# A DeltaNet scan over chunks of 128 tokens, restated in 64-token sub-chunks with two heads stacked on the partitions

## The chip, the cores and the metric

The kernel runs on one core of one Trainium2 chip. The metric is the device time of one launch in microseconds: the median of three runs before the change is 1980.43 us (1977.72 to 1982.88).

## The reference, cut to what matters

One layer of a hybrid trunk over a prompt of 1024 tokens and a sample of 32 tokens (width 1024): a joint input projection, eight gated DeltaNet heads of 64 with a causal convolution, eight stick-breaking attention heads, an output projection, an MLP of 4096 and a gated embedding. The change touches the DeltaNet rule alone:

```python
gcum = jnp.cumsum(gc, axis=-1)
decay = jnp.exp(jnp.where(causal, gcum[..., :, None] - gcum[..., None, :], -jnp.inf))
a_mat = jnp.where(strict, jnp.einsum('nbhid,nbhjd->nbhij', kb, kc) * decay, 0.0)
sol = lax.linalg.triangular_solve(a_mat + jnp.eye(l), rhs, left_side=True, lower=True, unit_diagonal=True)
qk = jnp.where(causal, jnp.einsum('nbhid,nbhjd->nbhij', qc, kc) * decay, 0.0)
def step(s, xs):
    v_new = u_i - jnp.einsum('bhld,bhde->bhle', w_i, s)
    o = (jnp.einsum('bhld,bhde->bhle', q_i * jnp.exp(g_i)[..., None], s)
         + jnp.einsum('bhij,bhje->bhie', qk_i, v_new))
    s = (s * jnp.exp(g_last)[..., None, None]
         + jnp.einsum('bhld,bhle->bhde', k_i * jnp.exp(g_last[..., None] - g_i)[..., None], v_new))
    return s, o
```

Each head carries a 64x64 state from chunk to chunk. Within a chunk the keys form a lower triangular matrix that must be inverted. The chunk length is free: any length gives the same result. All of it is float32.

## The kernel before, in words

The program runs in stages, one after another on all engines: input projection and convolution, stick-breaking attention (prompt, then sample), the DeltaNet scan, then output projection, MLP, embedding. The weight products take their operands as pairs of rounded halves, three PE passes each (tile_product); they are the part after the scan.

The scan works on CHUNKS = 9 chunks: chunk 0 is the sample (32 tokens), 1 to 8 are the prompt in pieces of 128 tokens. Tokens stand on partitions in the matrices of a chunk (128x128 for each of eight heads), channels in the transposed keys and queries (head pairs, 64 rows each). The order is written out by hand for each engine in a loop over i from -3, in which stages of several chunks are interleaved:

- chunk i+3: squares, square sums (square_sums, PE L2106), logs and norms on ACT, unit_norms (DVE L1581), decay_differences (DVE L1570, one operation per head);
- chunk i+2: products of keys (key_products, PE L2112), key_matrix on DVE (L1599), decayed keys and queries (L1589, L1590 on DVE, L933, L934 on POOL), turns of keys and values (L2135, L2137), products of queries (L2112 again). SP writes the key matrix to DRAM (blocks_out, L733) and reads back its 16x16 diagonal blocks as 64 lanes (L737). DVE inverts these on lanes (lanes_begin, lanes_middle, lanes_end, L1630 to L1666). SP scatters the inverses and their transposes into scratch of zeros (L742, L743) and reads whole matrices d_t and d_x back (L747, L750);
- chunk i+1: three levels double the inverted blocks from 16 to 128. A level is a product of the key matrix with d_t (L2207, last one L2256), a mask on ACT (L1244, L1258, L1273), a product that completes d_t (L2213) and one that completes d_x (L2220, last one L2264);
- chunk i: products_of_state (L2152, L2154), rest_of_values (DVE L1680), solved_values (PE L2171), new_values (DVE L1686), state_change (PE L2181), new_state (DVE L1691), outputs (PE L2190), norm of outputs, turn_outputs (PE L2200), rounding into act_hi and act_lo.

Iterations -3 to -1 are the prologue. In the last one the first tile of the output projection is interleaved. On PE every product of a head is one matmul with float32 operands; the profile shows two records for each, and one for a transpose. SP handles all loads of the scan in program order in one queue: blocks_out(i+2), sums_in(i+3), blocks_in(i+2), z_in, conv_v_in, conv_qk_in. A wait at one of them holds all behind it.

PSUM banks: key and query products put even heads into one bank and odd heads into the next (group, value and output use h % 2).

## Time and profile before

| | |
|---|---|
| median of 3 runs | 1980.43 us (1977.72 to 1982.88) |
| the profiled execution, its span | 1980.4 us |
| PE busy | 1826.4 us (92%) |
| DVE busy | 806.4 us (41%) |
| ACT busy | 522.2 us (26%) |
| POOL busy | 620.3 us (31%) |
| scan | about 648 to 992.7 us |

Busy time counts an engine's instructions from start to end; a busy PE is not a PE at its peak. In a timeline each row is a group of like instructions: start, length, engine, line, operation, outputs and inputs, shapes, and in brackets the idle time before it and what ended it. The clock column is the granted TensorE clock as a share of 2.4 GHz; it has two levels, 0.50 (1.2 GHz) and 1.00. Most of the profiled time lies after the scan, where PE streams weight products.

### The profile page before, as it was taken

The page shows a single profiled execution, that of the slowest core. Times are in us where ns is not written, and L with a number is a line of the kernel's source. Part 1 is how long each engine was busy: PE and PEld are TensorE (multiplying, and loading weights), DVE is VectorE, ACT ScalarE, POOL GpSimd, SP SyncE. Part 2 cuts the span into 40 slices and gives each one's busy share as a digit, 9 for nine tenths or more (in the row PEclk, how much of TensorE's full clock was granted, in tenths as well). Part 3 has the DMA queues.
Part 4 walks back from the last instruction along what each step waited for, and adds up shares of the span by engine and source line. Part 5 has one row for each costly group of instructions (what it writes and reads, how often), then busy time and mean ns, then how long its engine had stood idle before and what let it go on. Part 6 is the DMA issues. An engine that isn't in the chain of part 4 may idle for free.

```text
span 1980.4 us, 29352 instructions
## 1 busy us (share of the span) xinstructions
PE 1826.4 (92%) x12590; PEld 1728.3 (87%) x12590; DVE 806.4 (41%) x1031; ACT 522.2 (26%) x987; POOL 620.3 (31%) x337
## 2 busy tenths in 40 slices
PE   4999999989998468887999999999999999999998
PEld 4989989977776258777899999999999999999898
DVE  5552125558996455656213322212222222225432
ACT  4222122337776233443213201010101010103211
POOL 4132223312340112123053434443444344332430
PEclk9999999999999578888799999999999999999999
DMA  5121322132003443342232111111111111111121
GB/s 166 44 71 39 108 66 76 55 118 67 1 1 107 105 102 94 89 107 53 52 93 75 43 53 44 43 43 54 43 43 43 54 43 43 43 53 61 51 61 46
DMA packets 197663, 126.50 MB, mean 64 GB/s; under 512 B 39024, under 2 KB 190980, under 8 KB 197540
## 3 DMA queue, kind: packets, MB, share of 16 engines
q1 hardware_dynamic: 188112, 111.69, 19.5%
q10 hardware_dynamic: 9428, 13.02, 1.8%
q8 instruction: 96, 1.57, 0.3%
q14 instruction: 27, 0.22, 0.0%
HBM read 100.07 MB, written 24.62 MB: 63 GB/s over the span
## 4 chain that ended last, share of the span: by engine, by line
PE 75%; DVE 14%; issue 4%; ACT 4%; DMA 2%; POOL 1%; SPq 0%; ACTq 0%; DVEq 0%; POOLq 0%
PE psum L2074 41%; PE psum L1892 8%; PE psum L2388 5%; PE psum L1861 3%; PE psum L1862 3%; PE psum L1863 3%; DVE act_lo_plain L1527 3%; PE psum L2207 2%; DVE act_hi_plain L1528 2%; DVE area L1630 1%; PE psum L2106 1%; PE psum L1944 1%; PE psum L2407 1%; DVE area L1467 1%; DVE act_lo L1764 1%
## 5 line engine op out<-in xcount | busy, mean ns | idle before, releaser
L2074 PE MATMUL psum<-act_hi,w_round 128*128 128x352 f32 x1920 | 369.8, 326 | 0.5 <-DVE act_lo L1764 0.5
L911 POOL TENSOR_TENSOR w_round<-w_plain,ones 128x1024 fp32r<-128x1024 f32 x80 | 173.8, 2173 | 533.1 <-DMA w_plain<-in_w_up_dram 231.2
L2074 PEld LDWEIGHTS psum<-act_hi,w_round 128*128 128x128 f32 x1920 | 321.8, 190 | 1.4 <-DVE act_lo L1764 0.8
L2074 PE MATMUL psum<-hid_hi,w_round 128*128 128x352 f32 x1344 | 260.0, 324 | 0.4 <-DVE hid_lo L1794 0.4
L2074 PEld LDWEIGHTS psum<-hid_hi,w_round 128*128 128x128 f32 x1344 | 224.9, 188 | 0.7 <-DVE hid_lo L1794 0.7
L1771 DVE TENSOR_TENSOR area<-psum,area 128x1056 f32<-128x1056 f32 x72 | 90.5, 1257 | 311.3 <-PE psum L2074 311.3
L2074 PE MATMUL psum<-act_lo,w_round 128*128 128x352 f32 x960 | 208.0, 325 | 0.0
L912 POOL TENSOR_TENSOR w_round<-w_plain,w_round 128x1024 fp32r<-128x1024 f32 x80 | 198.5, 2481 | 6.3
L1386 ACT ACTIVATE hid_hi<-area 128x1056 fp32r<-128x1056 f32 x28 | 30.4, 1088 | 592.5 <-DVE area L1787 592.5
L1861 PE MATMUL psum<-w_round,act_hi 128*128 128x256 f32 (+1 forms) x576 | 166.3, 289 | 6.6 <-POOLq L863 3.6
L2074 PEld LDWEIGHTS psum<-act_lo,w_round 128*128 128x128 f32 x960 | 164.4, 189 | 0.0
L1862 PE MATMUL psum<-w_round,act_hi 128*128 128x256 f32 (+1 forms) x576 | 163.6, 284 | 0.0
L1863 PE MATMUL psum<-w_round,act_lo 128*128 128x256 f32 (+1 forms) x576 | 162.6, 282 | 0.0
L2074 PE MATMUL psum<-hid_lo,w_round 128*128 128x352 f32 x672 | 144.8, 324 | 0.0
L1787 DVE SCALAR_TENSOR_TENSOR area<-psum,area 128x1056 f32<-128x1056 f32 x32 | 40.2, 1257 | 240.1 <-PE psum L2074 235.1
L860 POOL TENSOR_TENSOR w_round<-w_plain,ones 128x2048 fp32r<-128x2048 f32 x14 | 50.5, 3609 | 254.2 <-PE psum L1863 163.2
L2074 PEld LDWEIGHTS psum<-hid_lo,w_round 128*128 128x128 f32 x672 | 114.0, 188 | 0.0
L1861 PEld LDWEIGHTS psum<-w_round,act_hi 128*128 128x128 f32 (+1 forms) x576 | 104.6, 182 | 7.9 <-issue 3.7
L1892 PE MATMUL psum<-act_hi,w_round 128*128 128x352 f32 x576 | 109.1, 324 | 0.0
L1863 PEld LDWEIGHTS psum<-w_round,act_lo 128*128 128x128 f32 (+1 forms) x576 | 105.0, 182 | 0.4
L1862 PEld LDWEIGHTS psum<-w_round,act_hi 128*128 128x128 f32 (+1 forms) x576 | 104.5, 181 | 0.4
L1527 DVE TENSOR_TENSOR_SCAN act_lo_plain<-act_lo_plain,w_plain 128x128 f32<-128x128 f32 (+7 forms) x64 | 88.3, 1380 | 23.5 <-ACT act_hi_plain L1096 22.7
(294 smaller groups left out, 2911.0 us busy)
## 6 DMA issues: line engine op xcount, KB each, us to landing
w_plain<-in_w_up_dram SPq DMA_DIRECT2D x32, 512.0 KB, 4.1
w_plain<-in_w_down_dram SPq DMA_DIRECT2D x32, 512.0 KB, 3.4
w_plain<-in_w_in_dram SPq DMA_DIRECT2D x14, 1024.0 KB, 5.6
conv_scratch<-area ACTq DMA_DIRECT2D x12, 512.0 KB, 2.7
w_plain<-decay_scratch SPq DMA_DIRECT2D x9, 512.0 KB, 3.5
area<-t_scratch SPq DMA_DIRECT2D x9, 512.0 KB, 4.2
area<-x_scratch SPq DMA_DIRECT2D x9, 512.0 KB, 5.5
area<-in_x_prompt_dram SPq DMA_DIRECT2D x8, 512.0 KB, 3.2
```

The lines of the kernel that those rows point to most:

```text
L860: own.link(pool.tensor_tensor(hi, w_raw[:, slot, :], ones[:, 0:1].to_broadcast([P, BLK]), ALU.mult))
L911: own.link(pool.tensor_tensor(hi, ring_raw(n), ones[:, 0:1].to_broadcast([P, RB]), ALU.mult))
L912: pool.tensor_tensor(lo, ring_raw(n), hi.bitcast(F32), ALU.subtract).then_inc(ring_split, 1)
L1527: own.link(dve.tensor_tensor_scan(back, back, starts, 0.0, ALU.mult, ALU.max))
L1771: dve.tensor_tensor(h3, chunks_of(bank_set(tile)), h3, ALU.add).then_inc(drained, 1)
L1787: dve.scalar_tensor_tensor(out=by_chunk(wide[:, n % 2, :]), in0=chunks_of(bank_set(tile)), scalar=0.0, in1=by_chunk(wide[:, 2, :]), op0=AL ...
L1861: pe.matmul(out, hi[:, k, cols], w_h(k), start=(k == 0), stop=False)
L1862: pe.matmul(out, hi[:, k, cols], w_l(k), start=False, stop=False)
L1863: last = pe.matmul(out, lo[:, k, cols], w_h(k), start=False, stop=(k == K - 1))
L1892: last = pe.matmul(bank(base + c)[0:rows, 0:CH], w(k), a[:, k, CH * c:CH * (c + 1)], start=(k == 0 and w is lhs_hi and a is hi), stop=(k = ...
L2074: last = pe.matmul(bank(bank_set(tile) + c)[:, 0:CH], w(k), a(k)[:, CH * c:CH * (c + 1)], start=(begins and k == ks[0] and w is w_h and a ...
L2388: last = pe.matmul(bank(c)[:, 0:CH], w(k), a[:, k, CH * c:CH * (c + 1)], start=(k == 0 and w is w_h and a is act_hi), stop=(k == KT - 1 an ...
```

## The change

A chunk of 128 tokens (or of 32, padded to 64) is split into sub-chunks of HD = 64 tokens, g = 0 and 1. Two heads are stacked on the partitions (index u), so that a matrix tile is [128, m, 64] with m = 4g + k: half u of the partitions holds head 2k + u. Every product of a head takes rows of half u and writes rows of half u of one bank (place). Elementwise operations on matrices of 128x1024 become 128x512. The inverse has two levels (16 to 32 on 64x64 products, 32 to 64 on 32x32 products); the third is gone. The state advances once per sub-chunk, step(q, g), twice per iteration, and alternates between two buffers. Turns become products with the identity, two per 128x128 piece and half. decay_differences is split: the subtraction runs on POOL (raw_differences), DVE takes the minimum with a mask. Several tiles have three buffers in place of two, d_gb and d_cn two in place of one. key_matrix is made one iteration earlier (chunk i+3), output norms one later (chunk i-1). d_t and d_x come back in four transfers (two halves each) under one semaphore, blocks_back, for which first_matrices waits. z comes in four transfers. SP's order changes: sums first, blocks_out last; the ring of weight blocks 2 to 4 is loaded in iteration 6 in place of after the scan, and POOL splits three of its blocks in the last iterations in place of two. For the sample, token sums and betas are laid out for the halves by small products before the scan.

```diff
-        d_dt = carve(area, 0, 2, H, P)
+        d_dt = carve(area, 0, 2, M2, HD)
...
+        def step(q, g):
+            return 2 * q - 1 + g if q else 0
+        def steps_to(q):
+            return 2 * q + 1
+        STATES = steps_to(CHUNKS - 1)
+        def state(n):
+            return d_s[:, (n - 1) % 2] if n else d_sin[:, 0]
+        def next_state_of(n):
+            return d_s[:, n % 2] if n else d_sin[:, 1]
...
+                sp.dma_start(scratch, zeros).then_inc(scratch_cleared, 16)
             sp.wait_ge(g_stored, 16)
             sums_in(0)
             sp.wait_ge(kc_turned, 2)
@@ -725,13 +749,15 @@
             sp.wait_ge(so_split, 2)
             for u in range(2):
                 sp.wait_ge(z_stored[u], 16 * NTT)
+            sp.dma_start(d_sin[:, 0], state_of["in"]).then_inc(s_loaded, 16)
 
             def blocks_out(q):
 
-                n = size(q)
                 sp.wait_ge(at_made, q + 1)
-                sp.dma_start(at_scratch[0:n, :, 0:n], d_at[0:n, q % 2, :, 0:n]).then_inc(at_dumped, 16)
-                sp.wait_ge(at_dumped, 16 * (q + 1))
+                for u in range(2):
+                    sp.dma_start(at_scratch[u, 0:HD, 0:mats(q)], d_at[HD * u:HD * (u + 1), q % 3, 0:mats(q)])\
+                      .then_inc(at_dumped, 16)
+                sp.wait_ge(at_dumped, 32 * (q + 1))
                 if q:
                     sp.wait_ge(scattered, 32 * q)
                 sp.dma_start(d_lane[:, 0:LB * LB].rearrange("l (r c) -> l r c", c=LB), at_lanes).then_inc(gathered, 16)
@@ -742,46 +768,45 @@
                 sp.dma_start(t_lanes, d_lane_t.rearrange("l (r c) -> l r c", c=LB)).then_inc(scattered, 16)
                 sp.dma_start(x_lanes, d_lane[:, 0:LB * LB].rearrange("l (r c) -> l r c", c=LB)).then_inc(scattered, 16)
...
-                if 0 <= i + 2 < CHUNKS:
-                    blocks_out(i + 2)
-                if 1 <= i + 3 < CHUNKS:
-                    sums_in(i + 3)
-                if i < 0:
-                    if i + 4 >= 2:
-                        conv_v_in(i + 4)
-                    conv_qk_in(i + 4)
-                    if i == -1:
-                        z_in(0)
+                if i + 4 < CHUNKS:
+                    sums_in(i + 4)
+                if i >= 0:
+                    if i == 0:
+                        sp.wait_ge(consts_made, 6)
+                    z_in(i)
                 if 0 <= i + 2 < CHUNKS:
                     blocks_in(i + 2)
-                if i >= 0:
-                    if i + 1 < CHUNKS:
-                        z_in(i + 1)
-                    if i + 4 < CHUNKS:
-                        conv_v_in(i + 4)
-                        conv_qk_in(i + 4)
+                if 2 <= i + 4 < CHUNKS:
+                    conv_v_in(i + 4)
+                if i + 4 < CHUNKS:
+                    conv_qk_in(i + 4)
+                if i + 3 < CHUNKS:
+                    blocks_out(i + 3)
                 if i == 1:
                     sp.wait_ge(s_new, 2)
-                    sp.dma_start(state_of["sample"], d_sin).then_inc(s_stored, 16)
-            sp.wait_ge(s_new, 1 + CHUNKS)
...
+            def raw_differences(q):
+                m = mats(q)
+                pool.wait_ge(gb_loaded, 32 * (q + 1))
+                pool.wait_ge(at_made, q)
+                gc = gc_all[:, chunk(q), 0:m].unsqueeze(2).to_broadcast([P, m, HD])
+                tt(d_db[:, 0:m], d_gb[:, q % 2, 0:m], gc, ALU.subtract).then_inc(dtb_made, 1)
...
-                for h in range(H):
-                    last = dve.scalar_tensor_tensor(out=d_db[0:n, h, 0:n], in0=d_gb[0:n, h, 0:n],
-                                                    scalar=gc_all[0:n, chunk(q), h:h + 1], in1=causal[0:n, 0:n],
-                                                    op0=ALU.subtract, op1=ALU.min)
-                last.then_inc(diff_made, 1)
+                m = mats(q)
+                dve.wait_ge(dtb_made, 2 * q + 1)
+                bound = causal[:].unsqueeze(1).to_broadcast([P, m, HD])
+                tt(d_db[:, 0:m], d_db[:, 0:m], bound, ALU.min).then_inc(diff_made, 1)
...
+            def place(b, u, m):
+                return bank(b)[half(u), HD * m:HD * (m + 1)]
...
+            def keys_on_state(q, g):
+                n = step(q, g)
+                pe.wait_ge(kg_made, q + 1)
+                pe.wait_ge(s_new, n + 1)
+                if n == 0:
+                    pe.wait_ge(s_loaded, 16)
+                for k in range(WT):
+                    for u in range(2):
+                        last = pe.matmul(place(5, u, k), d_kg[half(u), q % 3, WT * g + k], state(n)[half(u), k],
+                                         start=True, stop=True)
+                last.then_inc(ks_ready, 1)
...
+            def second_matrices(q):
+                pe.wait_ge(t16_made, q + 1)
+                for m in range(mats(q)):
+                    for u in range(2):
+                        top, rest = slice(HD * u, HD * u + 32), slice(HD * u + 32, HD * (u + 1))
+                        last = pe.matmul(bank(0)[rest, HD * m:HD * m + 32], d_at[top, q % 3, m, 32:HD],
+                                         d_t[top, q % 2, m, 0:32], start=True, stop=True)
+                last.then_inc(m_ready, 1)
```

PE's loop after the change (code of the new kernel):

```python
            for i in range(-3, CHUNKS + 1):
                now, two, final = 0 <= i < CHUNKS, 0 < i < CHUNKS, i == CHUNKS - 1
                if now:
                    keys_on_state(i, 0)
                if final:
                    pe.wait_ge(m_made, level(i, 1))
                    pe.wait_ge(qt_made, CHUNKS)
                    pe.wait_ge(x_made, level(i, 1))
                    heads_part([WT], True)
                if 0 <= i + 1 < CHUNKS:
                    first_matrices(i + 1)
                if now:
                    solved_values(i, 0)
                if 0 <= i + 1 < CHUNKS:
                    first_inverse(i + 1)
                if now:
                    state_change(i, 0)
                    outputs(i, 0)
                if i + 3 < CHUNKS:
                    square_sums(i + 3)
                if two:
                    keys_on_state(i, 1)
                if final:
                    heads_part([WT + 1], False)
                if i >= 1:
                    turn_outputs(i - 1)
                if 0 <= i + 1 < CHUNKS:
                    second_matrices(i + 1)
                if two:
                    solved_values(i, 1)
                if 0 <= i + 2 < CHUNKS:
                    turn_keys(i + 2)
                    query_products(i + 2)
                if 0 <= i + 1 < CHUNKS:
                    second_inverse(i + 1)
                if two:
                    state_change(i, 1)
                    outputs(i, 1)
                if final:
                    heads_part([WT + 2, WT + 3], False)
                if i + 3 < CHUNKS:
                    key_products(i + 3)
```

How the rows of an iteration move. PE, a steady iteration before, from the products of the state (L2152) on; names: 2207 level products, 2213 d_t, 2220 d_x, 2171 solved values, 2181 state change, 2190 outputs, 2106 square sums.

```order
L2152 MATMUL psum<-area 128x64 x8
L2154 MATMUL psum<-area 128x64 x8
L2112 MATMUL psum<-w_plain 128x128 x8
L2207 MATMUL psum<-area 128x128 x8
L2171 MATMUL psum<-area 128x64 x8
L2213 MATMUL psum<-area 128x128 x8
L2220 MATMUL psum<-area 128x128 x8
L2181 MATMUL psum<-area 64x64 x8
L2207 MATMUL psum<-area 128x128 x8
L2190 MATMUL psum<-area 128x64 x8
```

The same place now: state product (L2163), first matrices (L2219), solved values (L2172), d_t and d_x of the first level (L2227, L2233), state change (L2181), outputs (L2193, L2197), square sums (L2116), and the state product of the second sub-chunk.

```order
L2163 MATMUL psum<-area 64x64 x8
L2219 MATMUL psum<-area 64x64 x16
L2172 MATMUL psum<-area 64x64 x8
L2227 MATMUL psum<-area 64x64 x16
L2233 MATMUL psum<-area 64x64 x16
L2181 MATMUL psum<-area 64x64 x8
L2193 MATMUL psum<-area 64x64 x8
L2197 MATMUL psum<-area 64x64 x8
L2116 MATMUL psum<-w_plain,halves 128x512 x2
L2163 MATMUL psum<-area 64x64 x8
```

Products of 128 columns are gone but for the square sums, which moved between the two state steps, ahead of the second state product; the key products moved from here to the iteration's end.

SP's queue, a steady iteration before (L733 dump, L737 gather, L742 and L743 scatter, L747 and L750 returns):

```order
L733 DMA at_scratch<-area 128x8x128
L737 DMA area<-at_scratch 64x16x16
L651 DMA w_plain<-decay_scratch 128x1024
L742 DMA t_scratch<-w_plain 64x16x16
L743 DMA x_scratch<-area 64x16x16
L747 DMA area<-t_scratch 128x8x128
L750 DMA area<-x_scratch 128x8x128
L657 DMA area<-z_scratch 128x512
L644 DMA w_plain<-conv_scratch 128x4x128
L637 DMA w_plain<-conv_scratch 128x8x128
```

And now (L768, L769 scatter; L774, L779 returns; L758 dump; L763 gather):

```order
L671 DMA w_plain<-decay_scratch 64x512 x2
L682 DMA area<-z_scratch 64x4x64 x4
L768 DMA t_scratch<-w_plain 64x16x16
L769 DMA x_scratch<-area 64x16x16
L774 DMA area<-t_scratch 64x8x64 x2
L779 DMA area<-x_scratch 64x8x64 x2
L660 DMA w_plain<-conv_scratch 128x4x128
L653 DMA w_plain<-conv_scratch 128x8x128
L758 DMA at_scratch<-area 64x8x64 x2
L763 DMA area<-at_scratch 64x16x16
```

Dump and gather moved behind the scatter and returns of the chunk before. Ten transfers became seventeen, and those that carry the matrices of heads or z move rows of 64 elements.

## Rows read from the trace of the kernel before

**Rows 1.** The profile's page, header and granted clock of PE in 40 slices
```profile
span 1980.4 us, 29352 instructions
...
PEclk9999999999999578888799999999999999999999
```

**Rows 2.** Busy time by stretch: PE, PEld, DVE, ACT, POOL, then clock, DMA share, GB/s
```profile
680.00:720.00 40.00, 18.29 (x154) 14.51 (x152) 17.28 (x31) 7.45 (x14) 5.88 (x5) 0.61 0.46 119
...
789.37:823.92 34.55, 29.39 (x257) 25.70 (x257) 20.04 (x42) 13.62 (x29) 6.46 (x6) 0.85 0.37 98
...
992.70:1040.00 47.30, 47.29 (x301) 47.16 (x302) 5.61 (x5) 7.41 (x8) 23.70 (x11) 0.96 0.29 81
```

**Rows 3.** Timeline of PE: start us, us, engine, line, operation, records, idle before
```profile
740.55 1.11 PE L2152 MATMUL psum<-area 64*128 64x64 f32 x16
...
808.68 1.14 PE L2264 MATMUL psum<-area 64*64 64x64 f32 x16
...
882.61 2.05 PE L2207 MATMUL psum<-area 128*128 128x128 f32 x16
...
890.43 0.69 PE L2181 MATMUL psum<-area 128*64 128x64 f32 x16 [0.36 <-DVE area L1686]
...
947.46 1.97 PE L2152 MATMUL psum<-area 64*128 64x64 f32 x16
```

**Rows 4.** Timeline of PE, groups at the low clock
```profile
801.01 3.75 PE L2106 MATMUL psum<-w_plain,halves 128*128 128x512 f32 x4 [3.13 <-DVE area L1704]
...
943.71 1.96 PE L2264 MATMUL psum<-area 64*64 64x64 f32 x16
```

**Rows 5.** Busy time of single microseconds around the pause, columns as rows 2
```profile
800.00:801.00 1.00, 0.00 (x0) 0.02 (x1) 0.96 (x3) 0.00 (x0) 0.00 (x0) 0.50 0.14 17
...
807.00:808.00 1.00, 1.00 (x18) 0.93 (x17) 0.20 (x1) 0.41 (x2) 0.00 (x0) 1.00 1.20 296
```

**Rows 6.** Timeline of PE, sample attention and its last turn
```profile
640.92 0.65 PE L2023 MATMUL psum<-w_plain,act_hi_plain 128*32 128x64 f32 x32
...
645.56 0.65 PE L2052 MATMUL psum<-ident,act_hi_plain 32*64 32x32 f32 x16 [0.34 <-ACT act_hi_plain L1167]
```

**Rows 7.** Timeline of DVE, parts of the iterations at 789 and 824
```profile
795.59 1.01 DVE L1630 TENSOR_TENSOR area<-area 64x512 f32<-64x512 f32 x1
...
800.78 2.18 DVE L1570 SCALAR_TENSOR_TENSOR area<-w_plain,gc_all,causal 128x128 f32<-128x128 f32 x8
...
820.77 0.68 DVE L1589 TENSOR_TENSOR area<-w_plain 64x512 f32<-64x512 f32 x1 [4.07 <-ACT w_plain L1224]
821.47 1.67 DVE L1590 TENSOR_TENSOR area<-w_plain 64x512 f32<-64x512 f32 x1
...
825.03 0.07 DVE L1658 MEMSET area<- 64x16 f32 x1
...
825.91 0.42 DVE L1691 TENSOR_TENSOR area<-psum,w_plain 128x256 f32<-128x256 f32 x1
...
827.50 0.28 DVE L1634 TENSOR_REDUCE area<-area 64x32 f32<-64x128 f32 x1
```

**Rows 8.** Timeline of ACT, the four first masks
```profile
818.19 1.48 ACT L1244 ACTIVATE area<-psum,odd 32x128 f32<-32x128 f32 x4 [5.75 <-PE psum L2207]
```

**Rows 9.** Timeline of SP's DMA issues: scatter and first return
```profile
799.57 0.59 SPq L742 DMA_DIRECT2D t_scratch<-w_plain  x1
...
802.82 0.36 SPq L747 DMA_DIRECT2D area<-t_scratch  x1
```

**Rows 10.** DMA issues of the scan, median us from issue to landing
```profile
area<-t_scratch SPq DMA_DIRECT2D x9, 512.0 KB, 4.2
area<-x_scratch SPq DMA_DIRECT2D x9, 512.0 KB, 5.5
...
at_scratch<-area SPq DMA_DIRECT2D x8, 512.0 KB, 3.2
...
area<-at_scratch SPq DMA_DIRECT2D x9, 64.0 KB, 2.7
```

More of the change, by code:

```diff
@@ L2260, in last_inverse @@
[L2260 to L2286 removed]
+                pe.wait_ge(at_made, q + 1)
@@ new lines, in outputs @@
+            def outputs(q, g):
+                n = step(q, g)
+                pe.wait_ge(qg_made, q + 1)
+                pe.wait_ge(qt_made, q + 1)
+                if q:
+                    pe.wait_ge(on_read, q)
+                for k in range(WT):
+                    for u in range(2):
+                        pe.matmul(place(6, u, WT * g + k), d_qg[half(u), q % 3, WT * g + k], state(n)[half(u), k],
+                                  start=(g == 0 and k == 0), stop=False, skip_group_check=True)
+                for k in range(WT):
+                    for u in range(2):
+                        last = pe.matmul(place(6, u, WT * g + k), d_qt[half(u), q % 3, WT * g + k], d_vn[half(u), k],
+                                         start=False, stop=True, skip_group_check=True)
+                if g == subs(q) - 1:
+                    last.then_inc(o_made, 1)
@@ new lines, in first_inverse @@
+            def first_inverse(q):
+                pe.wait_ge(m_made, level(q, 0))
+                for m in range(mats(q)):
+                    for u in range(2):
+                        last = pe.matmul(place(0, u, m), d_x[half(u), q % 3, m], d_m[half(u), m], start=True, stop=True)
+                last.then_inc(t_ready, 1)
+                if q:
+                    pe.wait_ge(x_made, level(q - 1, 1))
+                for m in range(mats(q)):
+                    for u in range(2):
+                        last = pe.matmul(place(1, u, m), d_m[half(u), m], d_x[half(u), q % 3, m], start=True, stop=True)
+                last.then_inc(x_ready, 1)
```

851 lines of the change are left out of this document (377 added, 474 removed).

## The prediction

> **What bounds the kernel now.** Read first the page's header and clock line [rows 1], then the busy time in stretches [rows 2]. PE is busy in nearly all of 992.7 to 1040 us and stays so until the end; the change does not touch that part, it only starts earlier or later. The DeltaNet scan fills 648 to 992.7 us. Its steady part repeats: PE is busy 29.4 of 34.6 us of one iteration (85%), DVE 20.0, ACT 13.6, POOL 6.5 [rows 2]. The prologue is another matter: between 680 and 720 us PE is busy 18.3 of 40 us, since there each step waits for the one before. So two numbers matter: the length of an iteration, which PE's own work sets now, and the latency of the chain through the blocks' inverses, which sets the prologue. Iteration 1 starts at 740.55 us and iteration 7 at 947.46 (both are the first products with the state) [rows 3], which is 34.5 us per iteration.
>
> The PE timeline [rows 3] gives prices. A float32 product is two records. At the full clock a group of 16 records takes 2.05 us where both operands are 128 wide (128 ns a record), 1.14 us for 64x64 products on one tile (71 ns), and 0.69 us for 64-column products whose column halves alternate (43 ns). Two halves that alternate thus run beside each other. At half clock (0.50, which is 1.2 GHz) the 64x64 group takes 1.96 us, 122 ns a record [rows 4].
>
> The clock: PE is idle for 3.13 us before the square sums at 801.01 (after DVE L1704); the granted clock is 0.50 at 800 and 1.00 from 807 on, with PE busy since 801.01 [rows 4, 5]. It loses this in each iteration.
>
> **The change, part by part.**
>
> *Price of a product.* All products of a head become 64x64 on diagonal tiles, rows half u onto columns half u, u alternating. That form isn't in the scan before. Bounds: 71 ns if the tiles run one after another, 35 ns if they run in pairs (half of 71, and near the 43 of the alternating column halves). I take 36 at full clock and 61 at half (half of 122). The nearest row is the small turn at 645.56: four row groups alternating with two column halves, 16 records in 0.65 us at a clock of 0.50, so 40 ns [rows 6]; the attention's 32-column tiles take 20 ns [rows 6]. Both speak for pairs, and the first also writes one bank from two row groups.
>
> *Products per iteration.* Before, 252 records, most with 128-wide operands, and 4 for the square sums. Now: keys, queries, first matrices, both first inverses and turned outputs 32 each, turned keys and values 64, state products, solved values and state change 16 each for two sub-chunks, outputs 64; together 416 records of 64x64, and 64 of 32x32 for the second level (a third level is gone). PE: 416 x 0.036 + 64 x 0.030 + 1.9 (half of 3.75) = 18.8 us at full clock, 416 x 0.061 + 64 x 0.040 + 3.75 = 31.7 at half [rows 4]. The transposes cost more (two records per 64x64 piece instead of one per 128x128), all else less.
>
> A rule speaks against so many small products. The Trainium skill (TensorE: Matmul & The Clock Gate, What happens when you issue a matmul) says that with hardware decoding off the sequencer spends about 62 ns on each MATMUL. By it 484 records would take 30.0 us an iteration as an estimate; the sum goes by the rows instead. The trace disagrees: 20 ns a record at 640.92 [rows 6].
>
> *DVE.* decay_differences falls from 2.18 to 0.7 us (one operation of 512 elements, as 0.68 for the one at 820.77), the decayed queries from 0.68 + 1.67 to 0.7, the key and query matrices to half their size and time; three value and state steps run twice at 0.42 [rows 7]. The inverse of the 16-blocks on lanes is untouched. DVE goes from 20.0 to about 18, POOL from 6.5 to about 4.5, ACT stays under 13. None of them fills an iteration.
>
> *What is late next.* PE no longer bounds; a loop does. first_matrices(i+1) now waits for all four returning transfers of d_t and d_x. From that moment, F, in PE's and DVE's order: first matrices 32 x 0.061 = 1.95 (half clock, as PE has just waited); masks on ACT 1.48 [rows 8]; both first inverses 3.90; state change 16 x 0.061 = 0.98; the clock is back, outputs 1.15; square sums 1.9; second state product 0.6; rest_of_values on DVE 0.42; decay_differences 0.70; the lanes' first half 2.4 (825.03 to 827.78, less the 0.42 of the state step in it); new_values 0.42; the lanes' last half 3.95, from 795.59 to the scatter issued at 799.57 [rows 7, 9]; then SP: returns issued 802.82, so 3.25 [rows 9]; returns 4.5 (landing was 4.2 and 5.5 for 512 KB each [rows 10]; now four transfers of 128 KB, of as many pieces, each issued some 0.4 after the other: between 3.3 and 5.9). Together 27.6. To this, 0.7 for a dozen hand-overs (0.02 to 0.1 each in the timelines), and 1.0 because POOL's product falls into the lanes: of two DVE products of one size, 0.68 and 1.67, the second runs beside POOL [rows 7]. **29.3 us** per iteration instead of 34.5. The other loop, at_made through dump and gather (3.2 and 2.7 to land [rows 10], some 6.5 with the issues) to the lanes, has 10 us of slack, as the lanes begin 14 us after F. The recurrence itself is two rounds of 3 x 0.6 on PE and 3 x 0.42 on DVE, some 8 us; it doesn't decide.
>
> *Steady part.* Six intervals from F(2) to F(8); the last has no square sums and no differences: 5 x 29.3 + 26.6 = 173 instead of 207: 34 us saved.
>
> *Prologue.* SP's order now puts the next loads ahead of the waits for blocks. Key matrix 0 is made at about 654; dump and gather 6.5, lanes 7.5, scatter and returns 7.8 give F(0) = 676; matrices, masks, transposed product, first_transposed and differences 5.4, lanes 7.5, returns 7.8 give F(1) = 697; the same with state step and contention gives F(2) = 724 instead of 740.55: 16.5 us saved.
>
> *End.* Iteration 7 has no lanes: 16.5 us from F(8). Iteration 8 has two state steps but the same 12 products of the output tile between them, and the turning of outputs at the end: 20.5. From F(8) to the full stream of PE 37 us, against 45.2 before (947.46 [rows 3] to 992.7 [rows 2]): 8 to 8.5 saved. The weight blocks 2 to 4 are now loaded in iteration 6; PE didn't wait for them before, so nothing comes of it, nor from POOL splitting one block more.
>
> **Sum**: 34 (steady) + 16.5 (prologue) + 8.5 (end) = 59. The profiled execution has a span of 1980.4 us, the same as the median of the runs (1980.43), so the forecast is 1980.4 - 59 = **1921 us**.
>
> **Rivals.**
> 1. *Shorter loop*: the clock stays full and the returns take 3.3 us. F to F: 24.5 to 25 us, end near 1890. Against it: PE idles two or three times in each iteration (before F, at the masks, before the key products), some 7 of 29 us, and a 3 us pause cost the clock before.
> 2. *Half clock all through the iteration*: the loop takes 33 (outputs, square sums, state product and the hand-overs double), end near 1948. For it: the prologue, busy 46%, has a clock of 0.61 [rows 2]. Against it: at half clock PE would have 31.7 us of work in 33, and so dense a PE is granted the full clock.
> 3. *Diagonal tiles run one after another*, the rival on the other side. Two row groups write the same bank in every product of the new code (place() has no bank by half, before group() and value() had h % 2). At 71 ns PE has 416 x 0.071 + 64 x 0.043 + 1.9 = 34.2 us at full clock, and the loop through F, the masks and the key products leaves it idle for 4 to 5 more: 38 to 40 an iteration. Then 5 x 39 + 36 = 231, F(2) at 728, and an end of 43 us: 1002 instead of 992.7, so 1990. It decides from about 69 ns a record on, where the iteration reaches 38 us. The Trainium skill (TensorEngine Tiling (Array Packing), Restrictions and Gotchas) states that different row tiles cannot access the same PSUM bank simultaneously. By that rule the pairs would be impossible here and the time that of this rival; the turn at 645.56 speaks against it.
> 4. *Another wait takes PE's place at the same length*: the returns take 11 us instead of 4.5, being small pieces that queue with the loads of z and convolution. The loop is then 35.8 and F(2) comes at 743.5, so PE's full stream starts at 743.5 + 5 x 35.8 + 33 + 37 = 992.5. That is no change: within 0.3%, which is about what a measurement of this kernel can tell from none. Against it: 512 KB came back in 4.2 to 5.5 [rows 10].
>
> **How the numbers follow.** Forecast's case (loop of 27 to 31.5) 0.58, at 1905 to 1935. Rival 1 0.13, rival 2 0.16, rival 3 0.08, rival 4 0.05. Faster: 0.58 + 0.13 + 0.16 = 0.87; same 0.05; slower 0.08. The range goes from rival 1's time to a little beyond rival 2's, 1890 to 1950, and leaves out rivals 3 and 4 and the far end of rival 1.
>
> **What would show it.** The 64x64 groups of 16 records at 0.58 us or less at full clock (over 0.9 would be rival 3); PE busy for 60 to 75% of an iteration with a clock between 0.6 and 0.85; before first_matrices a PE wait of 1 to 3 us, released by the transfer of x_scratch; iterations of 27 to 31.5 us; iteration 1 near 724; the stages after the scan as long as before. The prediction is wrong if DVE fills the iteration, if first_matrices doesn't wait for DMA, or if the later stages change.

## The result, and the profile after

The changed kernel takes **1904.86 us** (median of 4 runs, 1901.27 to 1906.32), the kernel before 1979.88 beside it (4 runs, 1977.72 to 1982.88). The ratio is 0.9622, with a 95% interval of 0.9609 to 0.9636: 75 us, or 3.8%, faster. The forecast was 1921 in a range of 1890 to 1950, so the sign and the range hold, and the gain is 16 us larger than the sum said. The profiled execution took 1903.72 us. These are the header of its page and the granted clock of PE, to be read against [rows 1]:

```profile
span 1902.0 us, 33199 instructions
...
PEclk9999999998999878787999999999999999999999
```

The clock line dips to 7 in the scan and no longer to 5. Busy time by stretch (columns as in rows 2) shows how the balance moved:

```profile
680.00:720.00 40.00, 26.25 (x556) 21.78 (x555) 23.41 (x54) 16.08 (x37) 8.01 (x7) 0.80 0.32 66
...
778.43:806.02 27.59, 20.96 (x485) 18.79 (x485) 16.28 (x36) 10.72 (x24) 5.63 (x5) 0.75 0.38 85
806.02:834.49 28.47, 20.49 (x485) 18.46 (x485) 16.28 (x36) 10.71 (x24) 5.62 (x5) 0.74 0.38 86
834.49:860.71 26.22, 18.79 (x485) 16.76 (x485) 16.19 (x36) 10.71 (x24) 4.58 (x4) 0.83 0.36 75
```

The last three are whole iterations, from one first_matrices to the next. Against the 34.55 us of [rows 2], PE is busy 19 to 21 us in place of 29.4, that is 72 to 76% of the iteration, DVE 16.3 in place of 20.0. No engine fills an iteration: PE is waiting for something, and its timeline names it. Columns: start us, us, engine, line, operation, records, idle before and its releaser.

```profile
724.70 1.98 PE L2219 MATMUL psum<-area 64*64 64x64 f32 x32 [3.79 <-DMA area<-x_scratch]
...
806.02 1.97 PE L2219 MATMUL psum<-area 64*64 64x64 f32 x32 [2.24 <-DMA area<-x_scratch]
...
809.56 1.97 PE L2227 MATMUL psum<-area 64*64 64x64 f32 x32 [0.72 <-ACT area L1286]
811.33 1.92 PE L2233 MATMUL psum<-area 64*64 64x64 f32 x32
813.03 0.77 PE L2181 MATMUL psum<-area 64*64 64x64 f32 x16
...
814.67 1.98 PE L2116 MATMUL psum<-w_plain,halves 128*128 128x512 f32 x4
816.58 0.68 PE L2163 MATMUL psum<-area 64*64 64x64 f32 x16
817.10 1.10 PE L2208 MATMUL psum<-ident,area 64*64 64x64 f32 x32
818.13 0.69 PE L2241 MATMUL psum<-area 32*32 32x32 f32 x32
...
828.41 1.97 PE L2125 MATMUL psum<-area 64*64 64x64 f32 x32 [4.01 <-DVE area L1593]
...
860.71 1.98 PE L2219 MATMUL psum<-area 64*64 64x64 f32 x32 [2.70 <-DMA area<-x_scratch]
...
888.55 1.97 PE L2219 MATMUL psum<-area 64*64 64x64 f32 x32 [7.38 <-DMA area<-x_scratch]
...
893.08 1.10 PE L2233 MATMUL psum<-area 64*64 64x64 f32 x32
894.02 0.63 PE L2181 MATMUL psum<-area 64*64 64x64 f32 x16
```

L2219 is first_matrices; F(q) is the moment at which it starts for chunk q. F(2) is at 724.70 and F(8) at 888.55: six intervals of 27.3 us on average, each entered after a wait of PE for the transfer of x_scratch. Prices stand here too. Thirty-two records on the diagonal tiles take 0.94 us from one group's start to the next at full clock (L2233 starts at 893.08, L2181 at 894.02), which is 29 ns a record; at half clock 1.77 us (809.56 to the start of L2233 at 811.33), 55 ns. The 32x32 products take 0.62 us for 32 records (from L2241's start to that of the next group at 818.75), 20 ns.

DVE and SP, the rest of the same loop (columns as above):

```profile
817.31 0.42 DVE L1692 TENSOR_TENSOR area<-area,psum 128x256 f32<-128x256 f32 x1 [1.94 <-PE psum L2163]
817.65 0.68 DVE L1585 TENSOR_TENSOR area<-area,causal 128x512 f32<-128x512 f32 x1
818.29 0.07 DVE L1670 MEMSET area<- 64x16 f32 x1
...
824.73 0.37 DVE L1678 COPY w_plain<-area 64x256 f32<-64x256 f32 x1
```
```profile
825.12 0.60 SPq L768 DMA_DIRECT2D t_scratch<-w_plain  x1
825.76 0.67 SPq L769 DMA_DIRECT2D x_scratch<-area  x1
828.39 1.27 SPq L774 DMA_DIRECT2D area<-t_scratch  x2
829.71 2.08 SPq L779 DMA_DIRECT2D area<-x_scratch  x2
```

DVE waits for the second state product, does the value step, the minimum of the differences and the lanes without a pause, SP scatters at 825.12 and issues the returns at 828.39, and PE goes on at 834.49. The returns take 6.1 us from first issue to F, and the four issues alone 3.4. This is the longest of the six intervals: in the others the returns take 5.0 to 5.5 us and, but for one, the issues 2.6.

**Where the 75 us are.** Marks are F(2), F(8) and the first turn of the last outputs (L2327 at 918.89 now, L2339 at 992.71 before, the start that [rows 2] has for PE's full stream); the kernel before is read at its first products with the state, 740.55 and 947.46. The steady six intervals take 163.9 us in place of 206.9 [rows 3]: 43.0. F(2) stands at 724.70 in place of 740.55: 15.9. From F(8) to the mark it is 30.3 us in place of 45.3: 14.9. Together 73.8. What is left of the 78.4 us between the two spans, 4.6, lies behind the mark, where PE has the same products in both kernels: 987.7 us before, 983.1 now. Part of the 78.4 is a difference between executions, since the medians differ by 75.0 only. A time is 1.7 to 1.8 us longer than its span in every run, so the traced execution of the kernel before took about 1982.1, 2.2 over its median. But the traces of all thirteen kernels with the change, those of the experiments below included, have 980.6 to 983.6 us behind the mark. There is one trace of the kernel before, so whether the change has a share in the 4.6 is open.

### The profile page after: what moved, and what is told of

It is laid out like the page before. It is cut to its first block, busy times and chain, and to the rows that moved or that the text cites. A ratio compares the mean times of both kernels' runs of the same rounds, so it can differ in the third digit from the quotient of the medians.

```text
span 1902.0 us, 33199 instructions
## 1 busy us (share of the span) xinstructions
PE 1738.7 (91%) x14512; PEld 1648.3 (87%) x14512; DVE 767.2 (40%) x988; ACT 502.4 (26%) x970; POOL 615.0 (32%) x340
## 4 chain that ended last, share of the span: by engine, by line
PE 73%; DVE 13%; DMA 4%; issue 4%; ACT 2%; SPq 2%; POOL 1%; ACTq 0%; DVEq 0%; POOLq 0%
PE psum L2090 42%; PE psum L1902 8%; PE psum L2376 5%; DVE act_lo_plain L1544 3%; PE psum L1871 3%; PE psum L1872 3%; PE psum L1873 3%; DVE act_hi_plain L1545 2%; DVE area L1642 1%; DMA area<-x_scratch 1%; DMA x_scratch<-area 1%; PE psum L1954 1%; PE psum L2395 1%; DVE area L1482 1%; DVE area L1646 1%
```

## Experiments

Each kernel ran in 4 executions beside the kernel before. Ratios are to that kernel, with their 95% intervals.

### The same tile in a row

The theory was that pairing of diagonal tiles carries the gain, the rival that smaller matrices do. The edit reorders the products inside each group and nothing else (one loop of several that are changed alike):

```diff
-                for k in range(WT):
-                    for u in range(2):
+                for u in range(2):
+                    for k in range(WT):
```

> The changed kernel with its products in another order: in each group all eight (or four) products of half u = 0, then those of u = 1, in place of alternating. Same products, same waits. Theory (the two diagonal tiles run beside each other, and that is what made PE cheap): 16 records of 64x64 take 1.14 us at full clock instead of 0.47, PE has about 34 us of work per iteration and sets its length again, 37 to 40 us; total 1970 to 1995 us, the whole gain gone. Rival (small products are cheap in any order, and the gain is from the shorter waits and SP's new order): 16 records stay under 0.6 us, total within 10 us of 1905.

Measured: 1957.36 us (1954.79 to 1959.0), 0.9884 [0.9867, 0.9900], 52.5 us slower than the change. PE timeline of this kernel:

```profile
802.06 2.98 PE L2227 MATMUL psum<-area 64*64 64x64 f32 x29 [0.59 <-ACT area L1286]
...
813.50 1.67 PE L2208 MATMUL psum<-ident,area 64*64 64x64 f32 x29
815.10 1.09 PE L2241 MATMUL psum<-area 32*32 32x32 f32 x32
```

and its busy time over one iteration (columns as in rows 2):

```profile
797.19:831.57 34.38, 30.62 (x484) 28.58 (x484) 16.62 (x37) 10.71 (x24) 4.98 (x5) 0.75 0.30 68
```

With the same 484 records PE is busy 30.6 of 34.4 us. A record costs 55 ns at full clock (29 of them from 813.50 to 815.10) and 96 at half (29 from 802.06 to 804.84, where the next one starts), in place of 29 and 55. So diagonal tiles that alternate run at the pace of pairs, though both write the same bank. PE still waits for x_scratch, 0.4 to 2.2 us before F(3) to F(7), so the loop is the same one with longer groups in it: from F to the state change it takes 10.2 us, in place of 5.5 to 7.0. The time lies between the two expectations; theory had priced a record at 71 ns. So 52.5 of the 75 us are the pairing, by its order alone, and about 22 come with products on one tile too: this kernel is 1.2% faster than the one before. How these 22 divide between smaller matrices and the new order in SP's queue wasn't taken apart. The rival on the other side would have needed 69 ns a record; unpaired the tiles take 55 at full clock.

### Two waits of the loop, apart and together

In the loop read above, first_matrices needs only d_t, and the square sums stand ahead of the second state product for which DVE waits. The first edit gives the returns of d_x a semaphore of their own, for which first_inverse waits:

```diff
-                      .then_inc(blocks_back[q % 2], 16)
+                      .then_inc(x_back[q % 2], 16)
...
-                pe.wait_ge(blocks_back[q % 2], 64 * (q // 2 + 1))
+                pe.wait_ge(blocks_back[q % 2], 32 * (q // 2 + 1))
...
                 pe.wait_ge(m_made, level(q, 0))
+                pe.wait_ge(x_back[q % 2], 32 * (q // 2 + 1))
```

> The changed kernel with the returns of d_x under a semaphore of their own, waited for by first_inverse; first_matrices waits for d_t alone. Theory (the loop from the returned blocks through first_matrices, square sums, lanes, scatter and returns sets the iteration): first matrices start about 1.3 to 2.5 us earlier in each iteration, and 8 iterations give 10 to 18 us: 1887 to 1895. Rival (DVE's own work and its waits for PE set the iteration, and the wait for d_x only takes up slack): under 3 us.

The second puts square_sums(i + 3) behind solved_values(i, 1) in PE's order:

```diff
-                if i + 3 < CHUNKS:
-                    square_sums(i + 3)
                 if two:
                     keys_on_state(i, 1)
...
                     solved_values(i, 1)
+                if i + 3 < CHUNKS:
+                    square_sums(i + 3)
```

> The changed kernel with square_sums(i+3) on PE moved from ahead of the second state product to behind the second solved values. Theory (loop through the lanes): the second state product, and with it rest_of_values and the lanes, comes 1.9 us sooner; 5 steady iterations and the prologue's give 8 to 14 us: 1891 to 1897. Rival (the loop through norms, key matrix, dump and gather is as long): the later norms hold unit_norms, nothing is gained or up to 8 us lost.

> Both edits together: d_x waited for apart, square sums behind the second solved values. Alone they brought 10.5 and 9.4 us. Theory (both shorten one loop, at two places of it): they add, 1883 to 1888. Rival (they free the same slack, and another wait stops the second): 1891 to 1895.

Measured: d_x apart 1894.38 (1892.13 to 1901.09), 0.9580 [0.9558, 0.9602], 10.5 us under the change. Squares late 1895.42 (1894.99 to 1900.27), 0.9583 [0.9567, 0.9599], 9.4 under. Both 1886.64 (1885.48 to 1889.39), 0.9537 [0.9521, 0.9553], 18.2 under, so the two nearly add. All three lie in the range of their theory. PE timeline of the kernel with both (L2182 is the state change):

```profile
771.78 1.10 PE L2220 MATMUL psum<-area 64*64 64x64 f32 x32
...
796.65 1.15 PE L2220 MATMUL psum<-area 64*64 64x64 f32 x32 [0.65 <-DMA area<-t_scratch]
...
801.29 0.63 PE L2182 MATMUL psum<-area 64*64 64x64 f32 x16
...
820.77 1.15 PE L2220 MATMUL psum<-area 64*64 64x64 f32 x32 [0.43 <-DMA area<-t_scratch]
```

The intervals from F(2) to F(8) are 24.1 to 25.3 us, and before F(4) to F(7) the wait for the transfers is 0.65 us and less (1.9 before F(3), 5.9 before F(8)). Two edits that touch only the chain returns, first matrices, lanes made the run shorter, so that chain was the bound of the changed kernel.

The clock has a share in this. From F to the state change the chain runs on PE: 7.0 us at half clock (806.02 to 813.03), 4.6 at full clock (796.65 to 801.29). With both edits it takes 4.6 in four of the six intervals, in place of 5.5 to 7.0. That is 7.5 of the 15.1 us by which F(2) to F(8) is shorter, and with the squares alone it is 5.8 of 11.1. With d_x apart alone it is 0.2 of 5.8; there the returns take 3.7 to 4.2 us from first issue to F, and 7 us more are gained before F(2). So shorter pauses of PE seem to have given twice, by their own length and by the clock behind them; with one trace of each kernel the two can't be told fully apart.

### Keeping the clock up

The granted clock is 0.75 in an iteration of the change, and PE waits twice (4.0 us before the key products, 2.2 before the first matrices). The edit fills these places with products of ones into the free bank:

```diff
+            def fill(n):
+                for _ in range(n):
+                    pe.matmul(bank(0)[:, 0:P], halves[:], ones[:], start=True, stop=True)
...
+                if 2 <= i + 1 < CHUNKS:
+                    fill(8)
...
+                    if i > 0:
+                        fill(14)
```

> The changed kernel with extra products that nothing reads (ones by halves, 128x128, into bank 0) in PE's two pauses of each iteration: 14 before key_products, 8 before first_matrices. Theory (the pauses cost the clock, and first matrices, both first inverses and state change at 0.50 lie on the loop): granted clock over 0.95 in the scan, the loop shorter by 2.5 to 3.5 us an iteration, total 1885 to 1893. Rival (the clock falls anyway, or the fillers push what stands behind them by as much as they give): 1900 to 1915.

Measured: 1899.98 (1898.09 to 1901.48), 0.9598 [0.9582, 0.9614], 4.9 us under the change, and far less than expected. Busy time by stretch:

```profile
724.00:750.00 26.00, 21.72 (x517) 19.36 (x515) 15.98 (x36) 10.39 (x24) 5.00 (x5) 1.00 0.39 85
...
802.00:828.00 26.00, 21.60 (x528) 19.32 (x527) 15.81 (x36) 10.72 (x24) 5.29 (x5) 1.00 0.40 90
```

The clock is 1.00 in two of four such stretches, yet the six intervals from F(2) to F(8) take 158.1 us in place of 163.9. Of the loop's 27 us five to six are the returns, three the scatter and eight DVE, and their times didn't change with the clock. What did is the stretch from F to the state change, 7.8 us less over the six intervals, and 5.8 of it reached the steady part. The expectation had 2.5 to 3.5 us an iteration, as if this stretch ran at half clock throughout; in the changed kernel it did so in three of six. PE still waits 1.6 to 2.9 us for the transfer before F(3) to F(7), so the eight fillers ahead of the first matrices delay nothing.

### What comes next in the loop

Three further orders were tried on the kernel with both waits mended. First, output norms ahead of the first masks on ACT, and the normed output ahead of the first new values on DVE:

```diff
+                if i >= 1:
+                    output_norms(i - 1)
                 if 0 <= i + 1 < CHUNKS:
                     first_masks(i + 1)
```

> As the run before, and ACT's output_norms ahead of first_masks and squares, DVE's normed_output ahead of the first new_values, where DVE waits for PE. Theory (outputs wait for on_read, which stands behind squares and masks, and 1.4 us of DVE in the loop go into DVE's pause): 3 to 8 us below the run before. Rival (PE's outputs had no wait there, the loop does not pass through it): within 1 us of it.

Measured: 1883.28 (1879.87 to 1886.19), 0.9513 [0.9494, 0.9532], 4.9% under the kernel before and 21.6 us under the change: the fastest kernel of the study. Against the kernel it starts from it is 3.4 us, with intervals that overlap, so this last step isn't shown. The one trace of each doesn't bear out its mechanism either: F(2) to F(8) takes 149.8 us here and 148.7 there. One of its iterations by busy time (columns as in rows 2), and a wait in its DVE timeline, before the lanes, that the kernel it starts from didn't have in the steady part:

```profile
771.68:796.15 24.47, 16.44 (x484) 14.44 (x484) 17.32 (x38) 10.84 (x24) 5.71 (x5) 1.00 0.43 95
```

```profile
781.49 0.07 DVE L1671 MEMSET area<- 64x16 f32 x1 [1.92 <-DMA area<-at_scratch]
```

Then the lanes ahead of the second value step, on top of that:

> As the run before, and on DVE the lanes' first half ahead of the second rest_of_values, and decay_differences behind the lanes. Theory (the lanes are on the loop and wait only for program order, since the gathered blocks land about 6 us after first matrices start): lanes_made comes 2 to 4 us sooner per iteration, 8 to 16 us below the run before. Rival (the gather lands too late, or the second state step becomes the bound): 0 to 3 us, or slower.

Measured: 1889.39 (1888.42 to 1891.87), 0.9547 [0.9531, 0.9563], 6 us slower than without it. The PE and DVE timelines show why:

```profile
783.36 0.68 PE L2173 MATMUL psum<-area 64*64 64x64 f32 x16 [1.80 <-DVE area L1693]
...
788.32 1.97 PE L2151 MATMUL psum<-ident,area 64*64 64x64 f32 x32 [1.35 <-ACT w_plain L1253]
```
```profile
794.10 0.42 DVE L1704 TENSOR_TENSOR area<-psum,area 128x256 f32<-128x256 f32 x1 [6.00 <-PE psum L2182]
```

PE now waits for the value step that the lanes hold up, the square sums and turned keys behind it start later, and DVE stands 6.0 us for the state change. The lanes do end sooner: the scatter is issued 14.4 to 16.0 us after F, in place of 15.5 to 18.4. But F then comes 5.2 to 8.9 us after the first return is issued, with no wait for the transfer in these five of the six iterations, so PE's order bounds the loop there and no longer the returns. Fillers on top of it (ten and six) didn't help:

> As the run before, with unread products in PE's pauses (10 before key_products, 6 before first_matrices). Theory (the first fillers gained 5 and not 16 us because outputs then waited for normed_output, which is gone): now 6 to 14 us below the run before. Rival (the fillers stand in the way, as the pauses are shorter now): 0 to 5 us above it.

Measured: 1890.84 (1888.85 to 1894.08), 0.9561 [0.9545, 0.9577], 1.5 us above the kernel without them.

The wait for the gather was then attacked in SP's queue, on the fastest kernel:

```diff
-                if 2 <= i + 4 < CHUNKS:
-                    conv_v_in(i + 4)
-                if i + 4 < CHUNKS:
-                    conv_qk_in(i + 4)
                 if i + 3 < CHUNKS:
                     blocks_out(i + 3)
+                if 2 <= i + 4 < CHUNKS:
+                    conv_v_in(i + 4)
+                if i + 4 < CHUNKS:
+                    conv_qk_in(i + 4)
```

> g2_norms_early and, in addition, SyncE sends the dump of the key matrix and issues the gather ahead of the two convolution loads of the next chunk. In g2_norms_early the dump was issued at 771.75 us behind the two loads (0.62 and 0.51 us of issue) and the gather only at 777.82, 4.8 us behind the end of the dump's issue; VectorE then waited 1.92 us for the gather before the lane inverse. Theory (the gather is on the loop): the gather is issued 1.5 to 3 us earlier, VectorE's wait before the lane inverse goes, the loop shrinks from about 24.8 us by 0.5 to 1.5 us in each of some seven iterations, and the run takes 1873 to 1880 us. Rival (the convolution loads come late instead, since they now stand behind the wait for the dump; or the solved values' chain on TensorE is the bound): within 2 us of 1883.

Measured: 1900.11 (1898.19 to 1901.63), 0.9606 [0.9590, 0.9622]: 16.8 us slower, and outside both expectations. The SP timeline, then ACT and PE of the same kernel:

```profile
772.97 1.31 SPq L780 DMA_DIRECT2D area<-x_scratch  x2
781.15 1.27 SPq L759 DMA_DIRECT2D at_scratch<-area  x2
785.70 0.59 SPq L764 DMA_DIRECT2D area<-at_scratch  x1
786.34 0.66 SPq L661 DMA_DIRECT2D w_plain<-conv_scratch  x1
787.04 0.51 SPq L654 DMA_DIRECT2D w_plain<-conv_scratch  x1
```
```profile
793.46 1.06 ACT L1245 ACTIVATE w_plain<-w_plain 128x1024 f32<-128x1024 f32 x1 [9.24 <-DMA w_plain<-conv_scratch]
```
```profile
794.57 3.48 PE L2117 MATMUL psum<-w_plain,halves 128*128 128x512 f32 x4 [4.18 <-ACT w_plain L1245]
```

The dump waits for the key matrix until 781.15, and the loads now stand behind it in the one queue, though their data was written before the scan. The squares of the next chunk wait 9.24 us for them, the key matrix comes from those squares, and the next dump waits for the key matrix: by the order of the code this is a new loop through the queue, and these waits fit it. This was the named rival, but its price had been put at nothing.

### POOL beside the lanes

In the last interval of the change, F(7) to F(8), two tiny operations of the lanes take 0.95 and 2.20 us in place of 0.16. Each ends with the operation that POOL has beside it, at 871.49 and 873.93 where POOL's end at 871.47 and 873.90. DVE timeline of the change, and POOL's beside it:

```profile
870.54 0.95 DVE L1662 TENSOR_TENSOR area<-area 64x8 f32<-64x8 f32 x1
871.53 0.17 DVE L1663 TENSOR_TENSOR area<-area 64x8 f32<-64x8 f32 x1
871.73 2.20 DVE L1664 TENSOR_TENSOR area<-area 64x8 f32<-64x8 f32 x1
```
```profile
869.58 1.89 POOL L940 TENSOR_TENSOR w_round<-w_plain,ones 128x1024 fp32r<-128x1024 f32 x1
871.55 2.35 POOL L941 TENSOR_TENSOR w_round<-w_plain,w_round 128x1024 fp32r<-128x1024 f32 x1
```

The edit moves POOL's splits of weights one iteration later, on the changed kernel and on the one with the gather early:

```diff
-                if i >= CHUNKS - 3:
-                    split_ring(i - (CHUNKS - 3))
+                if i >= CHUNKS - 2:
+                    split_ring(i - (CHUNKS - 2))
...
-            for n in range(3, BLOCKS):
+            for n in range(2, BLOCKS):
```

> The changed kernel with the first pair of GpSimd splits of weights for the stage behind the scan moved from iteration 6 to iteration 7 (and the second from 7 to 8). In the changed kernel these two operations (1.89 and 2.35 us from 869.58) stand beside the lane inverse of chunk 8, in which one VectorE operation took 2.20 us instead of 0.16, and the first matrices of chunk 8 waited 7.38 us instead of 2.3 to 3.3. Theory (the two engines hold each other up there, and the lateness reaches TensorE's wait): the operation takes 0.16 to 0.3 us, the wait before the first matrices of chunk 8 is 3.5 to 5 us, and the run is 2 to 4 us shorter than the changed kernel, 1900 to 1903. Rival (the wait before chunk 8 is long because chunk 8's iteration has less work on TensorE, and the moved splits delay the stage behind the scan by as much): the operation is short, the run within 1 us of 1904.9.

> g5_gather_early with the first GpSimd split moved one iteration later as in x2_split_later. If both theories hold, their gains add: 1870 to 1877. If the splits' delay costs behind the scan what it saves in it, the same as g5_gather_early within 1.5 us.

Measured, on the change: 1902.46 (1900.33 to 1907.48), 0.9622 [0.9601, 0.9643]; on the other: 1899.87 (1897.71 to 1907.49), 0.9601 [0.9585, 0.9617]. DVE and PE of the first:

```profile
871.62 0.16 DVE L1664 TENSOR_TENSOR area<-area 64x8 f32<-64x8 f32 x1
```
```profile
886.30 1.97 PE L2219 MATMUL psum<-area 64*64 64x64 f32 x32 [7.26 <-DMA area<-x_scratch]
```

The operation is short again, and the interval F(7) to F(8) is 24.6 us in place of 27.8: the two stretched operations cost 2.8 of these 3.2. But PE's wait before F(8) is as long as before, 7.26 after 7.38: that wait is long because the iteration has less work for PE (no square sums, no key products), not because of POOL. And the whole run doesn't gain what the interval does: 2.4 us of the median on the change, 0.2 on the other, neither outside its interval. Between the two traces the span is 1.2 us shorter. F(7) is 1.0 later (861.71 for 860.71), F(8) to the mark takes 0.7 longer, and behind the mark it is 0.3: so most of the gain is lost inside the scan, and not behind it.

> g6_both with six products of ones of 128x128 ahead of the key products and six ahead of the first matrices, as in e4_filled_pauses but fewer. Theory (what keeps the clock at half in part of each iteration is the idle time of TensorE before these two places, and there is again idle time to fill): the mean granted clock of the run rises to about .97 to .98 and the run is 2 to 6 us shorter than g6_both. Rival (the chain over the transfers and VectorE sets the loop, so that faster products only wait longer; or the fillers delay the chain they stand in): the clock rises, the time stays within 1.5 us of g6_both or grows.

Measured, six and six fillers on the last kernel: 1896.68 (1894.55 to 1899.71), 0.9585 [0.9569, 0.9601], clock 0.973 in place of 0.963, and 3.2 us under the kernel without them. It lies in the range of the theory (2 to 6), but the intervals overlap.

## Why the prediction was right, and where it missed

**What bounds the kernel** was right on both sides of the change. PE's own work set the iteration before; now a loop from F through the masks, inverses, second state product, lanes, scatter and returns does. The two edits inside that loop show it, 10.5 and 9.4 us from moving a wait and a group. Iteration 1 near 724 came as forecast, and near enough PE's share (69 to 76%, 59% in the last interval, for 60 to 75) and the clock (0.74 to 0.83, once 0.87, for 0.6 to 0.85). The wait before first_matrices has the forecast releaser, but 1 to 3 us were forecast and it is 2.2 to 3.3 before F(3) to F(7), 3.8 and 7.4 at the ends. That the kernel before loses the clock in each iteration was said too strongly: after the same pause of 3.13 us its square sums at 835.55 took 1.96 us, the price at full clock.

**The price of a product** was too high. The sum took 36 ns at full clock and 61 at half; measured are 29 and 55. The step that mis-sized it divided a group's duration by its records. The last record's run to its end is in that duration: single records in the new timeline last 0.22 us at full clock. Of the 1.14 us for 16 records [rows 3] that leaves 0.92 for 15 steps, 61 ns and not 71, near the 55 that the experiment shows for one tile, and half of it is 31. So even the lower bound of 35 was too high. The 30 ns for a 32x32 record had no row behind it; it measured 20. A whole iteration at full clock costs PE 16.4 us (the stretch of the fastest kernel above), not 18.8.

**The loop of 29.3 us**, term by term for the interval that starts at 806.02, the longest of the six: F to the end of the first inverses 7.0 (forecast 7.3), state change and outputs 1.6 (2.1), square sums, second state product and hand-over 2.6 (2.5), DVE to the scatter 7.8 (7.9, and 1.0 for POOL), scatter to returns 3.3 (3.25), returns to F 6.1 (4.5). The total is 28.5 against 29.3. The **returns** were the one term put clearly too low: 6.1 is beyond the end of its own range, 5.9, and the other five, 5.0 to 5.5, are inside it. The four issues take 2.6 to 3.4 us, where the sum had counted 0.4 between them. Over all six intervals the largest term too high, beside POOL's, is **F to the end of the inverses**, 6.4 us on average for 7.3: the sum took the half clock for all of it, and the trace has 5.5, 6.4, 7.0, 7.0, 5.5 and 7.0. The **POOL contention** of 1.0 an iteration failed the other way: none of this interval's lane operations is stretched; it came in the last interval, beside the splits, and there cost 2.8. So the mean of 27.3 lies at the short end of 27 to 31.5, with errors of both signs in it: that it lies in the range is partly their cancelling. 43.0 us came from the steady part where 34 was said.

**The prologue** is right within 2 us: F(0), F(1), F(2) at 676.4, 698.8, 724.7 for 676, 697, 724, and 15.9 us for 16.5.

**The end** was mis-sized most: 14.9 us saved for 8 to 8.5. From F(8) to the next iteration's state product takes 12.8 us (forecast 16.5), the last iteration 17.6 (20.5). The prediction gives 16.5 and 20.5 without a sum, so which of their terms was too high stays open. The trace shows that PE runs here at a clock of 0.95, with groups of 16 at 0.47 us from start to start (894.02, 894.48, 894.95), where the sum's price is 0.58 at full clock and 0.98 at half. Before, part of the same place ran at half: groups of 16 records took 1.97 us at 972.29 and 3.51 at 978.70.

**The rivals.** Diagonal tiles one after another: excluded as the change stands (29 ns a record, where it needed 69), and even forced by the order of the code it gave 1957, not 1990. By the Trainium skill (TensorEngine Tiling (Array Packing), Restrictions and Gotchas) two row tiles can't access one bank at once; here alternating row tiles write different partitions of one bank at 29 ns a record against 55 on a single tile, so in time the rule isn't seen in this layout. The Trainium skill (TensorE: Matmul & The Clock Gate, What happens when you issue a matmul) gives 62 ns per MATMUL for hardware decoding off. They aren't seen either: the rows show 29 and 20. Which way of decoding was set no run here shows. Half clock throughout: no. A shorter loop at full clock: not so in the change. With the two waits mended it nearly came (24.1 to 25.3 an interval, and 1886.64 against the 1890 of that rival), by a shorter chain and a clock of 0.85 to 1.00 together; with the clock alone mended the run took 1899.98. Returns of 11 us: no, 5.0 to 6.1.

The **later stages** take the same as before but for 4.6 us of some 985, told above. The forecast also took the span of the traced execution, 1980.4, for a time; that is 1.7 us, less than the difference between two executions.

## What to carry to other kernels

Small products on diagonal tiles pay when consecutive records fall on different tiles: put the tile index innermost, and measure a record of that very form, since here 52 of the change's 75 us hung on the order of two loops. When an engine stops being the bound, write down the loop that takes its place and look in it for waits that are wider than their data (one semaphore over two arrays) and for groups that stand in it but don't belong to it; two such edits gave 18 us, the clock that came back with the shorter pauses included, where filling the pauses alone gave 5. The clock is worth what PE's groups on that loop take less, and no more. In a single DMA queue look at what a load whose data is ready stands behind: moving two such loads behind one wait for an engine cost 17 us.

## What was not expected of the hardware

- A float32 record of 64x64 on one tile costs 55 ns at full clock and 96 at half; on alternating diagonal tiles 29 and 55. For 32x32 it is 32 on one tile (815.10 to 816.12 for 32) against 20.
- An issue of a transfer with rows of 64 elements took 0.64 us on SP (1.27 for two) against 0.36 for one of the large returns before [rows 9], and four such issues in a row took 2.6 to 3.4 of the 5.0 to 6.1 us of the returns.
- A DVE operation on 64x8 elements took 2.20 us beside a POOL operation of 128x1024 and ended 0.03 us after it; without it the same one took 0.16. POOL's product of 128x512 at 821.41 stretched none of the lanes' operations.
- A granted clock of 0.87 to 1.00 in place of 0.74 to 0.87 in the steady iterations changed the run by a quarter of a percent: only the 4.6 to 7.0 us of each iteration that PE has between F and the state change got shorter.
